# Half-height products in pairs for the down half of a perceptron, the row halves changing banks midway

## The chip, the cores and the metric

The kernel runs on one core of one Trainium2 chip, as one program. Times are microseconds of device time. The figure that counts is the median over several runs; a profile of one execution shows where the time goes.

## The reference

A token sequence of 256 with model width 1024 goes through two layers, each of a mixer (attention variants) and a perceptron, then a differential attention layer. The change lies in the perceptron, which occurs twice:

```python
def sqrelu_mlp(u, w1, w2):
    return jnp.square(jax.nn.relu(u @ w1)) @ w2
...
for layer in range(DEPTH):
    u = rms_norm(h, attn_norm[layer])
    ...
    h = h + sqrelu_mlp(rms_norm(h, mlp_norm[layer]), mlp_w1[layer], mlp_w2[layer])
```

`w1` is 1024 x 4096 and `w2` is 4096 x 1024, both float32.

## The kernel before

Precision is kept by splitting: each float32 operand becomes a high part in the format fp32r and a low part (the rest), and a product is the sum of three: high by high, high by low, low by high. TensorE does these with a stationary operand of at most 128 x 128 (LDWEIGHTS) and a moving operand of at most 512 columns (MATMUL).

All weights come as one stream of units of 128 x 1024 values. SyncE loads a unit into one of 5 slots of `raw`; ScalarE writes its high part to one of 4 slots of `wh` (`act_split`, L453), VectorE its low part to `wl` (`dve_split`, L458); TensorE uses both and counts the unit off on the semaphore `w_used`, which frees the slot.

In a perceptron (`mlp`) the 4096 hidden values are 32 blocks of 128 (`FT`). For block f, `up` (L807, L810) makes the hidden values of all 256 tokens in one PSUM bank, `ptp` or `misc` in turn, with 8 products of 512 columns and 8 of 256. ScalarE and VectorE sum, square and split them into `hh` and `hl` (128 hidden values on the partitions, 256 tokens along the free dimension). `down` then multiplies them with the block's 128 rows of `w2` and adds to the four banks `acc[2 * half + t]`: token tile t (0 or 1) by output half (512 of the 1024 columns). It is two calls of `down_part`, one for each half: for each of the two tiles three products through `mm3` (L353 high by high, L354 high by low, L355 low by high), 12 in all, each of 128 rows and 512 columns.

The order on TensorE is written out by hand: up(0), up(1), then up(f + 2), down(f) for f from 0 to 29, of which the first 10 (`TPP`) are unrolled and 20 run in a hardware loop of 2 turns (`PASSES - 1`). The last two down halves (f = 30 and 31) are issued by `down_part` directly, interleaved with what follows. `down_ready` waits for the block's weights and hidden values. In the loop a wait's value comes from a register; `at` works it out from the turn number.

Elsewhere the kernel has products that use only 64 rows of the array: the index scores (`idx_scores`, L908) and the attention scores (`ab_scores`, L944, and `pe_scores`, L424), where a head has 64 values and lies on one half of the partitions. Those have plain float32 operands; TensorE runs each as two passes with a weight load of its own.

Of the kernel before, what the change touches and what calls it, by code (L numbers as in the profile page):

```python
# [13 lines left out]
P = 128  # L14
# [45 lines left out]
SPLIT = 4  # L60
# [11 lines left out]
FT = DFF // P  # L72
# [8 lines left out]
UPS = 20  # L81
U_P = U_L + UPS - 4
UNITS = U_L + UPS * STEPS
TPP, PASSES = 10, 3
# [108 lines left out]
def at(n, i=None, per=0):  # L193

    return n if i is None else i * per + n
# [9 lines left out]
def program(nc, x, stream, consts_d, cols_d, rows_d, sel_d, out):  # L205
    with ExitStack() as ctx:  # L206
        def sb(name, shape, dt=F32):
            return ctx.enter_context(nc.sbuf_tensor(name, shape, dt))

        def sem(name):  # L210
            return ctx.enter_context(nc.semaphore(name))
# [3 lines left out]
        wh = sb("wh", [P, SPLIT, UW], F32R)  # L215
        wl = sb("wl", [P, SPLIT, UW], F32R)
# [26 lines left out]
        hh = sb("hh", [P, 2, SEQ], F32R)  # L243
        hl = sb("hl", [P, 2, SEQ], F32R)
# [13 lines left out]
        acc = [ctx.enter_context(nc.psum_tensor(f"acc{i}", [P, 512], F32)) for i in range(4)]  # L258
# [8 lines left out]
        w_hi, w_lo, w_used = sem("w_hi"), sem("w_lo"), sem("w_used")  # L267
# [8 lines left out]
        z_turned, z_act, z_dve = sem("z_turned"), sem("z_act"), sem("z_dve")  # L276
        z_cross, z_summed, sqr_done = sem("z_cross"), sem("z_summed"), sem("sqr_done")
        hid_hi, hid_lo = sem("hid_hi"), sem("hid_lo")
        act_c, dve_c, pool_c = sem("act_c"), sem("dve_c"), sem("pool_c")
        roped = sem("roped")  # L280
        a_stat, a_rstd = sem("a_stat"), sem("a_rstd")
# [69 lines left out]
        def mm3(out_, ah, al, bh, bl, start, stop_):  # L351

            nc.tensor.matmul(out_, ah, bh, start=start, stop=False, skip_group_check=True)  # L353
            nc.tensor.matmul(out_, ah, bl, start=False, stop=False, skip_group_check=True)  # L354
            return nc.tensor.matmul(out_, al, bh, start=False, stop=stop_, skip_group_check=True)  # L355
# [408 lines left out]
        def _(pe):  # L764
            mm = nc.tensor.matmul
# [24 lines left out]
            def turn_h(b, h0, cc):  # L790

                pe.wait_ge(h_done, h0 + 2 * (cc // 2) + 2)
                pe_turn_block(pe, b, h, (cc,))

            def mlp(f0, u0, b, h0, next_b, next_h0):
                def up(f, u, i=None, blocks_k=range(KD)):

                    if blocks_k[0] == 0:
                        pe.wait_ge(w_lo, at(u + 1, i, UPS))
                    if blocks_k[0] == 0 and f0 + f >= 2:  # L800
                        pe.wait_ge(z_summed, at(f0 + f - 1, i, TPP))
                    for k in blocks_k:
                        if f == 0 and k % 2 == 0:
                            pe.wait_ge(lo_out, 4 * b + k // 2 + 1)
                        ks = slice(k * P, (k + 1) * P)
                        bank = (ptp, misc)[f % 2]
                        nc.tensor.matmul(bank[:, :], wh[:, u % SPLIT, ks],  # L807
                                         xhl[:, KD + k, :, :].rearrange("p a s -> p (a s)"),
                                         start=k == 0, stop=False, skip_group_check=True)
                        last = nc.tensor.matmul(bank[:, 0:SEQ], wl[:, u % SPLIT, ks], xh[:, KD + k, :],  # L810
                                                start=False, stop=k == KD - 1, skip_group_check=True)
                    if blocks_k[-1] == KD - 1:
                        last.then_inc(w_used, 1)

                def down_part(f, u, half, tiles=range(T), opens=False):

                    ws = slice(half * 512, (half + 1) * 512)
                    for t in tiles:
                        ts = slice(t * P, (t + 1) * P)
                        last = mm3(acc[2 * half + t][:, :], hh[:, f % 2, ts], hl[:, f % 2, ts],  # L820
                                   wh[:, u % SPLIT, ws], wl[:, u % SPLIT, ws], opens, f == FT - 1)
                    return last

                def down_ready(f, u, i=None):
                    pe.wait_ge(w_lo, at(u + 1, i, UPS))
                    pe.wait_ge(hid_lo, at(f0 + f + 1, i, TPP))

                def down(f, u, i=None):

                    down_ready(f, u, i)  # L830
                    down_part(f, u, 0, opens=f == 0)
                    down_part(f, u, 1, opens=f == 0).then_inc(w_used, 1)

                up(0, u0, blocks_k=range(4))
                turn_h(b, h0, 2)
                turn_h(b, h0, 3)
                up(1, u0 + 1, blocks_k=range(4))
                for ks in (range(4, 6), range(6, KD)):
                    up(0, u0, blocks_k=ks)
                    up(1, u0 + 1, blocks_k=ks)  # L840
                for f in range(TPP):
                    up(f + 2, u0 + 2 + 2 * f)
                    down(f, u0 + 3 + 2 * f)
                with pe.Fori(0, PASSES - 1) as i:
                    for f in range(TPP, 2 * TPP):
                        up(f + 2, u0 + 2 + 2 * f, i)
                        down(f, u0 + 3 + 2 * f, i)
                u = u0 + 2 * FT - 2
                down_ready(FT - 2, u)
                down_part(FT - 2, u, 0)  # L850
                down_ready(FT - 1, u + 1)
                down_part(FT - 1, u + 1, 0).then_inc(half_summed, 1)
                down_part(FT - 2, u, 1).then_inc(w_used, 1)
                down_part(FT - 1, u + 1, 1, (0,))
                turn_h(next_b, next_h0, 0)
                down_part(FT - 1, u + 1, 1, (1,)).then_inc(w_used, 1)
                turn_h(next_b, next_h0, 1)
# [10 lines left out]
            for cc in range(4):  # L868
                pe.wait_ge(x_in[cc // 2], 32)
                for c in range(2):  # L870
                    for t in range(T):
                        f = (2 * cc + c) * P
                        last = nc.tensor.transpose(opening[cc][:, c * SEQ + t * P:c * SEQ + (t + 1) * P],
                                                   h[:, t, f:f + P], ident)
# [200 lines left out]
            for k in range(4):  # L1075
                kv, uu = divmod(k, 2)
                u = U_CMP + k
                pe.wait_ge(w_lo, u + 1)
                for j in range(8):
# [3 lines left out]
                    last = mm3(misc[0:CG * N_CMP, kv * P:(kv + 1) * P], xw_h[:, cs], xw_l[:, cs],  # L1083
                               wh[:, u % SPLIT, ws], wl[:, u % SPLIT, ws],
                               uu == 0 and j == 0, uu == 1 and j == 7)
# [1561 lines left out]
```

## Time and profile before

| | |
|---|---|
| median of 3 runs | 913.39 us (913.18 to 915.85) |
| span of the profiled execution | 912.6 us, that is 0.8 us below the median |
| TensorE busy | 892.9 us, 98% |
| VectorE, ScalarE, GpSimd busy | 650.9, 515.4, 134.8 us (71%, 56%, 15%) |
| DMA | 146.40 MB, 160 GB/s mean |
| products on TensorE | 4781, each with a weight load |

The profile gives no time of the profiled execution other than its span. Matmuls are pipelined: the time shown for one is longer than the distance from one start to the next, and it is this distance that adds up. PE is TensorE's stream of products, PEld its weight loads.

### The profile page before, as it was taken

Reading aid. Unit: us, or ns where it says so; the run is one execution under the profiler, and the core shown is the slowest. Engines: PE = TensorE matmul, PEld = TensorE weight load, DVE = VectorE, ACT = ScalarE, POOL = GpSimd, SP = SyncE. Lnnn points to the kernel's source line nnn. Section 1 sums busy time; section 2 is a strip of 40 time slices with the busy share of each in tenths; the row PEclk is TensorE's granted clock in tenths of the full one; section 3 lists DMA queues with packets and bytes.
Section 4 is the critical chain, followed back from the end, with each engine's and each line's share of the span. In section 5 each row is a group of like instructions: output and inputs, shape, how many; then the busy total and the mean of one; then the engine's idle time right before and its main releaser. Section 6 shows DMA issues by size and latency. Waiting matters only on the chain. (4 is left out here: it accounts for less than half of the span.)

```text
span 912.6 us, 14857 instructions
## 1 busy us (share of the span) xinstructions
PE 892.9 (98%) x4781; PEld 738.5 (81%) x4781; DVE 650.9 (71%) x1306; ACT 515.4 (56%) x1019; POOL 134.8 (15%) x186
## 2 busy tenths in 40 slices
PE   8999999999999999998999999999999999999998
PEld 6878788888888888787888888888887778878876
DVE  4768757666666689787576666666887878777785
ACT  6653836444444466666464444444656766666573
POOL 2310300000000010365210000000430401400401
PEclk9999999999999999999999999999999999999999
DMA  9743144655555557101446555555464345454531
GB/s 353 237 148 110 39 148 155 201 194 188 185 184 189 190 173 233 46 2 47 141 141 222 189 185 185 187 192 192 142 208 162 137 140 169 153 177 148 161 116 47
DMA packets 40953, 146.40 MB, mean 160 GB/s; under 512 B 4544, under 2 KB 5056, under 8 KB 40896
## 3 DMA queue, kind: packets, MB, share of 16 engines
q1 hardware_dynamic: 40608, 145.43, 47.3%
q8 instruction: 34, 0.56, 0.2%
q10 hardware_dynamic: 288, 0.22, 0.1%
q14 instruction: 23, 0.19, 0.1%
HBM read 144.59 MB, written 1.05 MB: 160 GB/s over the span
## 5 line engine op out<-in xcount | busy, mean ns | idle before, releaser
L458 DVE TENSOR_TENSOR wl<-raw,wh 128x1024 fp32r<-128x1024 f32 x269 | 330.8, 1234 | 138.8 <-ACT wh L453 133.2
L453 ACT ACTIVATE wh<-raw 128x1024 fp32r<-128x1024 f32 x270 | 284.5, 1056 | 150.6 <-PE acc L355 126.0
L353 PE MATMUL acc<-wh,xhl 128*128 128x512 f32 (+1 forms) x472 | 190.6, 404 | 1.0 <-DVE wl L458 0.7
L355 PE MATMUL acc<-wh,xhl 128*128 128x512 f32 (+1 forms) x472 | 184.5, 391 | 0.0
L354 PE MATMUL acc<-wl,xhl 128*128 128x512 f32 (+1 forms) x472 | 183.8, 390 | 0.0
L353 PEld LDWEIGHTS acc<-wh,xhl 128*128 128x128 f32 x472 | 88.7, 188 | 25.3 <-issue 8.0
L355 PEld LDWEIGHTS acc<-wh,xhl 128*128 128x128 f32 x472 | 88.6, 188 | 19.2
L354 PEld LDWEIGHTS acc<-wl,xhl 128*128 128x128 f32 x472 | 88.8, 188 | 16.4
L355 PE MATMUL acc<-wh,hl 128*128 128x512 f32 x256 | 101.1, 395 | 0.0
L354 PE MATMUL acc<-wl,hh 128*128 128x512 f32 x256 | 100.9, 394 | 0.0
L353 PE MATMUL acc<-wh,hh 128*128 128x512 f32 x256 | 100.9, 394 | 0.0
L807 PE MATMUL ptp<-xhl,wh 128*128 128x512 f32 x256 | 91.0, 396 | 0.7 <-DVE hr L2012 0.7
L807 PE MATMUL misc<-xhl,wh 128*128 128x512 f32 x256 | 90.7, 395 | 0.0
L810 PE MATMUL ptp<-xhl,wl 128*128 128x256 f32 x256 | 71.0, 277 | 0.0
L810 PE MATMUL misc<-xhl,wl 128*128 128x256 f32 x256 | 70.9, 277 | 0.0
L502 POOL TENSOR_SCALAR st<-st 128x2 f32<-128x2 f32 x7 | 2.7, 386 | 420.4 <-ACT o_tok L495 243.6
L807 PEld LDWEIGHTS ptp<-xhl,wh 128*128 128x128 f32 x256 | 48.0, 187 | 13.0 <-issue 1.2
L353 PEld LDWEIGHTS acc<-wh,hh 128*128 128x128 f32 x256 | 47.9, 187 | 11.8
L355 PEld LDWEIGHTS acc<-wh,hl 128*128 128x128 f32 x256 | 47.9, 187 | 11.6
L807 PEld LDWEIGHTS misc<-xhl,wh 128*128 128x128 f32 x256 | 48.0, 187 | 11.3
L354 PEld LDWEIGHTS acc<-wl,hh 128*128 128x128 f32 x256 | 47.9, 187 | 8.9
L810 PEld LDWEIGHTS ptp<-xhl,wl 128*128 128x128 f32 x256 | 48.1, 188 | 1.4
(301 smaller groups left out, 1316.1 us busy)
## 6 DMA issues: line engine op xcount, KB each, us to landing
raw<-stream SPq DMA_DIRECT2D x270, 512.0 KB, 3.3
h<-x SPq DMA_DIRECT2D x4, 256.0 KB, 4.8
out<-h SPq DMA_DIRECT2D x3, 256.0 KB, 2.1
row<-rows SPq DMA_DIRECT2D x1, 700.0 KB, 11.2
probs<-sel SPq DMA_DIRECT2D x1, 512.0 KB, 10.1
cst<-consts SPq DMA_DIRECT2D x1, 507.0 KB, 9.5
out<-h SPq DMA_DIRECT2D x2, 128.0 KB, 2.0
col<-cols ACTq DMA_DIRECT2D x1, 154.5 KB, 4.1
```

The lines of the kernel that those rows point to most:

```text
L353: nc.tensor.matmul(out_, ah, bh, start=start, stop=False, skip_group_check=True)
L354: nc.tensor.matmul(out_, ah, bl, start=False, stop=False, skip_group_check=True)
L355: return nc.tensor.matmul(out_, al, bh, start=False, stop=stop_, skip_group_check=True)
L453: nc.scalar.activation(wh[:, u % SPLIT, :], raw[:, u % RAW, :], ACT.Copy).then_inc(w_hi, 1)
L458: nc.vector.tensor_tensor(wl[:, u % SPLIT, :], raw[:, u % RAW, :], wh[:, u % SPLIT, :].bitcast(F32), ALU.subtract).then_inc(w_lo, 1)
L502: chain_link(nc.gpsimd.tensor_scalar(dst, src, 1.0 / width, EPS, ALU.mult, ALU.add))
L807: nc.tensor.matmul(bank[:, :], wh[:, u % SPLIT, ks], xhl[:, KD + k, :, :].rearrange("p a s -> p (a s)"), start=k == 0, stop=False, skip_gr ...
L810: last = nc.tensor.matmul(bank[:, 0:SEQ], wl[:, u % SPLIT, ks], xh[:, KD + k, :], start=False, stop=k == KD - 1, skip_group_check=True)
```

## The change

`down` no longer calls `down_part`. The block's 128 hidden values are cut into rows 0 to 63 and 64 to 127, and each product into two of half the height. Of a pair, one runs on the array's lower rows for one token tile, the other on the upper rows for the other tile, into different banks. For each output half that makes three pairs (one for each of the three parts). After both output halves (`swap` 0), the row halves change tiles (`swap` 1), so that every tile gets both its halves of the sum. Before a row half adds to a bank that the other wrote, a wait on the new semaphore `part_done` sees to it that those products are complete. Such waits stand at the head of each of the four groups of six products: for swap 1 on the group two before, for swap 0 on the block before (on `w_used` for its second half, and for f = 0 none). `stop` is False throughout; `start` is set on the first products into each bank.

```diff
+        part_done = sem("part_done")
...
                 def down(f, u, i=None):
 
                     down_ready(f, u, i)
-                    down_part(f, u, 0, opens=f == 0)
-                    down_part(f, u, 1, opens=f == 0).then_inc(w_used, 1)
+                    before = (f0 // FT) * 3 * (FT - 2) + 3 * f
+                    for swap in range(2):
+                        for half in range(2):
+                            if swap == 1 or (f > 0 and half == 0):
+                                pe.wait_ge(part_done, at(before + (half + 1 if swap else 0), i, 3 * TPP))
+                            elif f > 0:
+                                pe.wait_ge(w_used, at(u - 1, i, UPS))
+                            for part, (x_, w_) in enumerate(((hh, wh), (hh, wl), (hl, wh))):
+                                for r in range(2):
+                                    t = r ^ swap
+                                    rows = slice(64 * r, 64 * r + 64)
+                                    last = mm(acc[2 * half + t][:, :], x_[rows, f % 2, t * P:(t + 1) * P],
+                                              w_[rows, u % SPLIT, half * 512:(half + 1) * 512],
+                                              start=f == 0 and part == 0 and swap == 0, stop=False,
+                                              skip_group_check=True)
+                            last.then_inc(w_used if swap == 1 and half == 1 else part_done, 1)
```

## Rows read from the trace of the kernel before

**Rows 1.** The page: span, busy time by engine, and slices of the span.
```profile
span 912.6 us, 14857 instructions
...
PE 892.9 (98%) x4781; PEld 738.5 (81%) x4781; DVE 650.9 (71%) x1306; ACT 515.4 (56%) x1019; POOL 134.8 (15%) x186
...
PEclk9999999999999999999999999999999999999999
```

**Rows 2.** Groups (busy, mean ns | idle before), 145 to 328 us; TensorE's wait (us, times, longest).
```profile
L458 DVE TENSOR_TENSOR wl<-raw,wh 128x1024 fp32r<-128x1024 f32 x64 | 78.3, 1225 | 39.8 <-ACT wh L453 38.0
...
L355 PE MATMUL acc<-wh,hl 128*128 128x512 f32 x128 | 50.5, 395 | 0.0
...
L353 PE MATMUL acc<-wh,hh 128*128 128x512 f32 x128 | 50.4, 394 | 0.0
...
PE ptp L807 <- DVE hr L2012: 0.3, 1, 0.3
```

**Rows 3.** Timeline of TensorE (start, duration in us), 202.5 to 206 us: one down half.
```profile
202.94 0.28 PE L810 MATMUL misc<-xhl,wl 128*128 128x256 f32 x1
203.06 0.39 PE L353 MATMUL acc<-wh,hh 128*128 128x512 f32 x1
203.28 0.39 PE L354 MATMUL acc<-wl,hh 128*128 128x512 f32 x1
...
205.85 0.40 PE L807 MATMUL ptp<-xhl,wh 128*128 128x512 f32 x1
```

**Rows 4.** Timeline of TensorE, 48.35 to 49.5 us: into `idx_scores`.
```profile
48.38 0.39 PE L354 MATMUL acc<-wl,xhl 128*128 128x512 f32 x1
48.61 0.39 PE L355 MATMUL acc<-wh,xhl 128*128 128x512 f32 x1
48.93 0.37 PE L908 MATMUL pair<-QK 64*128 64x128 f32 x1
48.94 0.37 PE L908 MATMUL misc<-QK 64*128 64x128 f32 x1
49.14 0.27 PE L908 MATMUL pair<-QK 64*128 64x128 f32 x1
...
49.25 0.38 PE L908 MATMUL pair<-QK 64*128 64x256 f32 x1
```

**Rows 5.** Timeline of the weight loads at the same place.
```profile
48.93 0.18 PEld L908 LDWEIGHTS pair<-QK 64*128 64x128 f32 x1 [0.35 <-issue]
48.93 0.18 PEld L908 LDWEIGHTS misc<-QK 64*128 64x128 f32 x1
49.03 0.19 PEld L908 LDWEIGHTS pair<-QK 64*128 64x128 f32 x1
```

**Rows 6.** Timeline of TensorE, 87 to 89 us: into and out of `ab_scores`.
```profile
87.01 0.33 PE L939 MATMUL acc<-decay,selr 128*128 128x256 f32 x1
87.27 0.37 PE L944 MATMUL pair<-QK 64*128 64x128 f32 x1
...
87.60 0.38 PE L944 MATMUL pair<-QK 64*128 64x256 f32 x1
...
87.82 0.38 PE L944 MATMUL pair<-QK 64*128 64x256 f32 x1
...
88.13 0.50 PE L353 MATMUL acc<-wh,xhl 128*128 128x512 f32 x1
88.46 0.40 PE L354 MATMUL acc<-wl,xhl 128*128 128x512 f32 x1
```

**Rows 7.** Timeline of TensorE, 67.44 to 68.2 us: transposes, then products.
```profile
67.22 0.60 PE L417 MATMUL pair<-cst,Y 128*128 128x128 f32 x4
67.58 0.48 PE L353 MATMUL acc<-wh,xhl 128*128 128x512 f32 x1
67.89 0.40 PE L354 MATMUL acc<-wl,xhl 128*128 128x512 f32 x1
```

**Rows 8.** Timeline of ScalarE, 202.5 to 203.4 us.
```profile
203.25 0.39 ACT L1442 ACTIVATE probs<-misc 128x256 f32<-128x256 f32 x1 [1.41 <-PE misc L810]
```

## The prediction

> **What bounds the kernel now.** I read the page first. TensorE is busy 98% of the span and its granted clock is 9 tenths or more in every slice, while VectorE is at 71% and ScalarE at 56% [rows 1]. So TensorE sets the pace; what has to be asked is whether that holds in the two perceptron stages, because an average can hide a stage with another limit. The groups of one perceptron (145 to 328 us) answer it: the three products of the down half stand there with 128 instructions each and no idle time before them [rows 2]. VectorE's costliest group there, the low part of the weights, has itself waited 39.8 us, nearly all for ScalarE's high part. TensorE's own waits in that stretch add up to 0.3 us [rows 2]. Here every nanosecond added to TensorE's stream lengthens the run, and every one taken away shortens it, up to the slack of the others.
>
> The timeline then gives the price of a down half. Its 12 products start at 203.06 us and the next up half starts at 205.85 [rows 3]: 2.79 us, or 233 ns for 512 columns. A product's shown duration, 0.39 us, is its way through the array, not its rate: the next starts after 0.23. I count starts, never durations.
>
> **What changes.** In 30 of the 32 hidden blocks of each perceptron (10 written out, 2 x 10 in the loop), so 60 times in all, `down` issues 24 half-height products in place of 12 full-height ones. The last two blocks keep `down_part`. Weight loads double from 12 to 24 and four waits come in. No transfer, no ScalarE, VectorE or GpSimd instruction changes.
>
> *The streaming.* Each half-height product streams as many columns as a full one, so 24 of them take the time of 12 only if two run at once. The kernel already has such pairs: in `idx_scores` the two heads of a pair lie on the two row halves. There the products of `pair` and `misc` start 0.01 us apart, and each next one 0.11 us later for 128 columns [rows 4] and 0.22 for 256 [rows 6]; their weight loads run two at once as well [rows 5]. So concurrency is real, and two loads every 0.11 us are sustained. But those are f32 products that take a column in about 0.86 ns (0.22 us over 256), against 0.455 ns (233/512) in the down half. Two streams at the full rate never occur in this trace. From below, nothing lets a pair be done before one full-height product would be: the least that I give it is the clock, 512 columns at 2.4 GHz, 213 ns. From above, if the two streams exclude each other at that rate, a pair takes 2 x 233 = 466. I take 233, since the f32 pairs show no mutual slowing whatever, and the 20 ns above 213 then stay. The term is 12 x 233 - 12 x 233 = 0. At best 12 x 60 x 20 ns = 14.4 us are gained; by exclusion 12 x 60 x 233 ns = 168 us are lost. In other words, nothing in the streaming is saved by design: the array's area times time is the same.
>
> *The change of height.* This is what I think decides. It happens twice in each new down half. Going in: the last full-height product before `idx_scores` starts at 48.61, its forerunner at 48.38 (0.23 apart), but the first half-height pair only at 48.93, so 0.32 instead of 0.23: 0.09 us. That pair then holds its place until 49.14, 0.21 us for 128 columns, where the following 128 columns take 0.11: 0.10 us [rows 4]. The weight loads tell why: the first is at 48.93, together with its product, whereas from the second on the load stands 0.11 us ahead of its product (49.03 for 49.14) [rows 5]. Not one weight load crosses the change of height, so the array empties and the load lies bare. Going out: the last half-height products start at 87.82, a pass of 256 columns as the one from 87.60, so the next was due at 88.04; it starts at 88.13 (0.09), and lasts until 88.46, 0.33 instead of 0.23 or 0.24 (0.10) [rows 6]. Both changes together: 0.09 + 0.10 + 0.09 + 0.10 = 0.38 us, and 0.01 for the second half that starts later. Another place gives an upper value for going in: from 87.01 to 87.27 after 256 columns, the width of the up half's last product, 0.26 where the up half shows 0.12 [rows 3, 6], so 0.14 in place of 0.09; part of it is that product's own wait for weights (it lasts 0.33, not 0.28). I take 0.39 per block, with 0.44 as upper end.
>
> Is it the height, and not the number format that changes at the same places? The last f32 transposes at full height, four from 67.22 at 0.11 each, run into an fp32r product at 67.58 and a next one at 67.89 [rows 7]. The transposes need until 67.66 and the product 0.23 more: 67.89. Format costs nothing; height does. 60 x 0.39 = 23.4 us, with nothing over it, since TensorE has no idle time in which to hide it.
>
> The Trainium skill speaks both ways here. "TensorEngine Tiling (Array Packing)", section Tiling Modes, holds against the change: going from one mode to another drains TensorE. "TensorE: Matmul & The Clock Gate", section Part 1, holds for it: a weight load is drawn ahead of running products if it goes to the background buffer. By the second, the two bare loads of 0.10 would vanish, 12 us of the 23.4, and the run would take 925; [rows 5] show the first load bare, so the trace sides with the first rule and I keep the whole.
>
> *The waits.* Each group of six products (three pairs) is followed by another on different banks, and the third one waits for the first. From the last pair of a group to the weight load of the group that waits lie three pairs, 0.70 us. A 256-column product that starts at 202.94 with 0.28 us shown is read by ScalarE at 203.25 [rows 3, 8]: the shown end plus 0.03. For 512 columns that makes 0.39 + 0.03 = 0.42 us, 0.28 less than 0.70. The two waits at the head of the down half look at a whole up half or more before. What is queued behind a waiting weight load is all of TensorE's stream, but the load is not due yet when it is released. TensorE's queue can also fill fast enough: a pair's four instructions, two loads and two products, go out every 0.11 us for 128 columns [rows 4, 5], and the new pairs have 0.23. I take nothing. If the queue does not run ahead past a wait, the two waits midway cost up to 0.42 - 0.23 = 0.19 us for the product to finish and 0.10 for the bare load, 0.29 each: 60 x 2 x 0.29 = 35 us.
>
> *Who is late next.* Slots of `wh` and `wl` come free 0.39 us later per block, but TensorE needs them 0.39 later too. VectorE, which waited already [rows 2], waits longer. Nothing is given back.
>
> Sum: 23.4 us on a profiled span of 912.6, 936.0. The median of the runs lies 0.8 above the span, so 936.8; I say 937.
>
> **Rivals.**
> *The streams hinder each other.* For it: no row shows two at 0.455 ns a column. Against it: f32 pairs go undisturbed, in separate banks. Full exclusion gives 913.4 + 23.4 + 168 = 1105; half of that, 1021. Chance 0.11.
> The Trainium skill, "TensorE: Matmul & The Clock Gate", section Part 3, gives 3.07x for four row tiles at 512 columns. An estimate from that page alone, a pair at 4/3.07 of 233 ns, would be 303 ns and 987 us in all; no row here shows it.
>
> *The waits bite.* Place: swap 1, both halves. Price up to 35 us, so 972; a third of it gives 949. It decides if a product's completion reaches the queue later than 0.70 us after its start. Chance 0.12.
>
> *The pair runs at the clock.* If the 20 ns over 213 come with the height, 14.4 us return: 922. For it: f32 pairs at 256 columns take 0.22, close to the clock. Against it: fp32r's excess is proportional to the columns, 0.12 for 256 in the up half. Chance 0.11.
>
> *No cost of the change, the other side.* Place: the first weight load of each down half and of the up half behind it, which would be drawn under the running products. Price: 23.4 us less, so 913.4, no change; with pairs at the clock 899. It decides below (2.7/60 =) 0.045 us per block. Against it: each change of height in [rows 4, 6] is paid for, while loads at one height are drawn ahead. Chance 0.06, split between no change (0.03) and faster (0.03).
>
> **How the numbers follow.** My forecast has 0.58, and the remaining 0.02 go to something unseen and slower. Being faster with the height's cost in place would need pairs below 233 - (23.4 + 2.7)/0.72 = 197 ns, under the 213 of the clock, so faster needs the last rival. A measurement of this kernel can tell about 0.3%, 2.7 us. Faster 0.03, same 0.03, slower 0.94. The range: low 922 for the pair at the clock; high 960, which takes in 0.44 per block (940) and most of the waits' cases. It leaves out the streams that hinder each other, the worst waits and the other side, some 0.2.
>
> **What would show it.** Right: a block's down half takes 3.18 us from its first product to the up half's first, not 2.79; inside it pairs 0.01 us apart, at 0.23 us; a gap of 0.09 and a first pair of 0.33 at its head, and a first up product of 0.33 behind it; TensorE's weight loads with idle time put down to "issue" there. Wrong: pairs at 0.21 or over 0.30; a stretched pair at the middle of the down half (the waits); a first weight load that starts ahead of its product. Most of all I would be wrong if two full-rate streams do not fit side by side.

## The result, and the profile after

The changed kernel takes 939.42 us (median of 4 runs, 939.18 to 939.62), beside 913.51 us for the kernel before in the same comparison. The ratio is 1.0276, with a 95% interval of 1.0259 to 1.0293. It is slower by 25.9 us. I had said 937, slower by 23.6.

The page after, answering to [rows 1]: TensorE is as full as before, at 9 tenths of its clock or more in every slice as before. The other engines have the instructions they had; VectorE and ScalarE are busy for the same time (GpSimd 136.1 us against 134.8).

```profile
span 937.4 us, 16421 instructions
...
PE 917.7 (98%) x5501; PEld 733.7 (78%) x5501; DVE 650.9 (69%) x1306; ACT 515.4 (55%) x1019; POOL 136.1 (15%) x186
...
PEclk9999999999999999999999999999999999999999
```

There are 720 products more (60 x 12) and 720 weight loads more, and the busy time shown for the loads fell from 738.5 to 733.7 us. So a count of instructions would have misled here: the two loads of a pair overlap, and the time that they share is counted once.

TensorE's timeline over one block, in time where [rows 3] are (start, shown duration in us; x2 folds two products into a row, here the two of a pair):

```profile
206.25 0.40 PE L808 MATMUL misc<-xhl,wh 128*128 128x512 f32 x1
206.49 0.28 PE L811 MATMUL misc<-xhl,wl 128*128 128x256 f32 x1
206.70 0.50 PE L843 MATMUL acc<-wh,hh 64*128 64x512 f32 x2
207.04 0.39 PE L843 MATMUL acc<-wl,hh 64*128 64x512 f32 x2
207.26 0.40 PE L843 MATMUL acc<-wh,hl 64*128 64x512 f32 x2
207.50 0.39 PE L843 MATMUL acc<-wh,hh 64*128 64x512 f32 x2
...
209.37 0.40 PE L843 MATMUL acc<-wh,hl 64*128 64x512 f32 x2
209.69 0.50 PE L808 MATMUL ptp<-xhl,wh 128*128 128x512 f32 x1
210.03 0.28 PE L811 MATMUL ptp<-xhl,wl 128*128 128x256 f32 x1
...
212.50 0.28 PE L811 MATMUL ptp<-xhl,wl 128*128 128x256 f32 x1
212.72 0.50 PE L843 MATMUL acc<-wh,hh 64*128 64x512 f32 x2
```

Read the starts. From 206.49 to the first pair it is 0.21 us, where the same step before is 0.12. The first pair holds its place for 0.34. From 207.04 to 209.37 there are ten steps of 0.233, the old pace. The duration shown for two products folded together, 0.39 or 0.40, is that of one alone, so the two of a pair start within about 0.01 us of each other. From the last pair to the up half it is 0.32, and the up half's first product holds for 0.34. The 0.50 shown for the two products behind a change, against 0.39 or 0.40, is the same delay seen from inside.

The weight loads at the head of the down half, answering to [rows 5]:

```profile
206.25 0.19 PEld L811 LDWEIGHTS misc<-xhl,wl 128*128 128x128 f32 x1
206.69 0.18 PEld L843 LDWEIGHTS acc<-wh,hh 64*128 64x128 f32 x2 [0.26 <-issue]
206.80 0.19 PEld L843 LDWEIGHTS acc<-wl,hh 64*128 64x128 f32 x2
207.04 0.19 PEld L843 LDWEIGHTS acc<-wh,hl 64*128 64x128 f32 x2
```

The load for the product of 206.49 is there at 206.25, one product ahead. The load for the first pair comes at 206.69, together with it. The next one is ahead again. Nobody is named as releaser of the 0.26 us before it: "issue" means that no other engine was waited for.

TensorE's loads over most of the first perceptron (145 to 330 us), in the view of the waits (us in total, times, longest):

```profile
PEld acc L843 <- issue: 7.8, 30, 0.3
PEld ptp L808 <- issue: 4.3, 11, 0.6
PEld misc L808 <- issue: 4.1, 11, 0.4
PEld ptp L808 <- DVE wl L459: 1.5, 4, 0.4
PEld misc L808 <- DVE wl L459: 1.5, 4, 0.4
```

The 30 idle stretches ahead of L843 are the 30 changes into the half height. The four rows below are the changes out of it (29 of them, and one stretch of 0.6 us before the first; the last change out lies just past 330 us). Two of them name VectorE for 4 changes each. The idle time is 0.37 us at every one of the 29, while VectorE's split had ended anything from 0.22 to 0.78 us before the load, so VectorE is not what was waited for.

### The profile page after: what moved, and what is told of

Same layout as the page of the kernel before. It is cut to its first block and busy times, and to the rows that moved or that the text cites. A ratio compares the mean times of both kernels' runs of the same rounds, so it can differ in the third digit from the quotient of the medians.

```text
span 937.4 us, 16421 instructions
## 1 busy us (share of the span) xinstructions
PE 917.7 (98%) x5501; PEld 733.7 (78%) x5501; DVE 650.9 (69%) x1306; ACT 515.4 (55%) x1019; POOL 136.1 (15%) x186
## 5 line engine op out<-in xcount | busy, mean ns | idle before, releaser
L843 PE MATMUL acc<-wh,hh 64*128 64x512 f32 x480 | 101.1, 418 | 0.0
L808 PE MATMUL ptp<-xhl,wh 128*128 128x512 f32 x256 | 95.2, 411 | 0.7 <-DVE hr L2027 0.6
L808 PE MATMUL misc<-xhl,wh 128*128 128x512 f32 x256 | 95.3, 411 | 0.0
L843 PE MATMUL acc<-wh,hl 64*128 64x512 f32 x480 | 95.1, 392 | 0.0
L843 PE MATMUL acc<-wl,hh 64*128 64x512 f32 x480 | 94.7, 391 | 0.0
L843 PEld LDWEIGHTS acc<-wh,hh 64*128 64x128 f32 x480 | 45.0, 184 | 23.4 <-issue 15.2
L843 PEld LDWEIGHTS acc<-wh,hl 64*128 64x128 f32 x480 | 45.0, 184 | 10.9
L843 PEld LDWEIGHTS acc<-wl,hh 64*128 64x128 f32 x480 | 45.0, 184 | 8.3
L1437 ACT ACTIVATE probs<-probs,nb 128x128 f32<-128x128 f32 (+1 forms) x96 | 42.3, 444 | 11.5 <-DVE nb L1965 11.5
```

The source lines that it names most:

```text
L808: nc.tensor.matmul(bank[:, :], wh[:, u % SPLIT, ks], xhl[:, KD + k, :, :].rearrange("p a s -> p (a s)"), start=k == 0, stop=False, skip_gr ...
L843: last = mm(acc[2 * half + t][:, :], x_[rows, f % 2, t * P:(t + 1) * P], w_[rows, u % SPLIT, half * 512:(half + 1) * 512], start=f == 0 an ...
L1437: last = s_.activation(pb[:, c0:c0 + n], pb[:, c0:c0 + n], ACT.Exp, scale=-1.0, bias=nbs[:, a, t:t + 1], accum_out=sus[:, a, t:t + 1])
```

## The experiments

Seven kernels ran. The figures of the changed kernel stand beside them: 939.42 us, ratio 1.0276. Each ratio is against the kernel before as it ran beside that experiment, 912.94 to 914.25 us, so differences between medians of two experiments are good to about 1 us.

**No change of height inside the loop.** The up half in pairs too.

```diff
                         bank = (ptp, misc)[f % 2]
+                        if f >= 2:
+                            for x_, n in ((wh, 2 * SEQ), (wl, SEQ)):
+                                for r in range(2):
+                                    rows = slice(64 * r, 64 * r + 64)
+                                    to = (bank, pair[f % 2])[r]
+                                    last = mm(to[:, 0:n], x_[rows, u % SPLIT, ks],
+                                              xhl[rows, KD + k, 0:n // SEQ, :].rearrange("p a s -> p (a s)"),
+                                              start=k == 0 and n > SEQ, stop=k == KD - 1 and n == SEQ,
+                                              skip_group_check=True)
+                            continue
```

> The down half stays as changed, and the up half of blocks 2 to 31 is cut into half-height pairs as well, the upper rows' products going to a bank of their own (pair), which nobody adds: the upper rows' half of the up sum is left out of the result. The array's height then changes only at the ends of the two perceptrons, not twice per block. If the change of height is what costs (0.39 us a block), 60 blocks give it back: 914 to 918 us, and no block shows a gap or a stretched first pair. If half-height pairs, doubled weight loads or the four waits cost something of themselves, the time stays at 939 us or rises, since there are more pairs than before and the same waits.

Measured: 915.13 us (913.42 to 921.51), ratio 1.0017 (0.9999 to 1.0036), no measurable difference from the kernel before. The down half of this kernel is the changed kernel's, with its 24 half-height products, its 24 loads and its four waits. Its timeline across the head of the down half:

```profile
203.28 0.39 PE L813 MATMUL pair<-xhl,wh 64*128 64x512 f32 x1
203.43 0.28 PE L813 MATMUL misc<-xhl,wl 64*128 64x256 f32 x1
203.51 0.28 PE L813 MATMUL pair<-xhl,wl 64*128 64x256 f32 x1
203.55 0.46 PE L853 MATMUL acc<-wh,hh 64*128 64x512 f32 x2
203.78 0.47 PE L853 MATMUL acc<-wl,hh 64*128 64x512 f32 x2
...
206.12 0.47 PE L853 MATMUL acc<-wh,hl 64*128 64x512 f32 x2
206.35 0.39 PE L813 MATMUL ptp<-xhl,wh 64*128 64x512 f32 x1
```

From 203.43 to 203.55 it is 0.12, from 203.55 to 203.78 0.23, and the whole down half takes 2.80 us (203.55 to 206.35), the 2.79 of [rows 3]. The gap and the stretched first pair are gone with the change of height. One thing about the pairs differs: their two products start 0.08 us apart, as the half-height products of the up half before them do (203.43 and 203.51), which is why 0.46 or 0.47 is shown for two. The pace is 0.233 all the same. This is the run that carries the explanation.

**Four changes of height per block instead of two.** Output half 0 at full height between the two swaps of output half 1.

```diff
+                    half = 1
+                    for swap in range(2):
+                        if swap == 1:
+                            down_part(f, u, 0, opens=f == 0)
+                            pe.wait_ge(part_done, at(before + 1, i, TPP))
+                        elif f > 0:
+                            pe.wait_ge(w_used, at(u - 1, i, UPS))
...
+                        last.then_inc(w_used if swap == 1 else part_done, 1)
```

> Only output half 1 is in half-height pairs; output half 0 stays at full height and stands between the two swaps, so a block changes height four times instead of twice, with half of the half-height products (12 of 24) and two waits fewer. If each change of height costs about 0.2 us: two more per block, 60 x 0.39 = 23 us more than the changed kernel, 963 us (960 to 967). If the cost goes with the number of half-height products, weight loads or waits, it is halved: 926 us.

Measured: 962.37 us, ratio 1.0524 (1.0507 to 1.0542): 22.95 us above the changed kernel, 0.38 us per block for two changes more. Half the half-height products and twice the changes give nearly twice the loss (5.2% against 2.8%), so the loss goes with the changes. The inner ones in its timeline:

```profile
204.57 0.40 PE L844 MATMUL acc<-wh,hl 64*128 64x512 f32 x2
204.90 0.50 PE L354 MATMUL acc<-wh,hh 128*128 128x512 f32 x1
205.25 0.39 PE L355 MATMUL acc<-wl,hh 128*128 128x512 f32 x1
...
206.17 0.40 PE L356 MATMUL acc<-wh,hl 128*128 128x512 f32 x1
206.50 0.49 PE L844 MATMUL acc<-wh,hh 64*128 64x512 f32 x2
206.83 0.40 PE L844 MATMUL acc<-wl,hh 64*128 64x512 f32 x2
```

Out: 0.33 and 0.35 where 0.23 is due; in: 0.33 and 0.33. The format is the same on both sides (fp32r), which [rows 4] and [rows 6] could not offer.

**No crossing, no waits.**

```diff
-                            if swap == 1 or (f > 0 and half == 0):
-                                pe.wait_ge(part_done, at(before + (half + 1 if swap else 0), i, 3 * TPP))
-                            elif f > 0:
-                                pe.wait_ge(w_used, at(u - 1, i, UPS))
...
-                                    t = r ^ swap
+                                    t = r
...
-                            last.then_inc(w_used if swap == 1 and half == 1 else part_done, 1)
+                    last.then_inc(w_used, 1)
```

> As changed, but the row halves keep their tiles in the second round, so no bank is ever written from both and the semaphore part_done and all four waits of a block are gone (half of each product's sum is left out and the other half counted twice). If the waits are hidden, as I forecast: 939 us, within 1.5. If they cost something: up to 35 us less, down to 905; a few us if the register arithmetic behind them is what slows the up half by the 0.05 us per block that I see in the profile and did not forecast.

Measured: 939.40 us, ratio 1.0272 (1.0255 to 1.0289). The four waits and the register arithmetic behind them cost nothing that can be measured, and they do not explain the slower up half either: in this kernel's trace it takes the same 3.02 us from its first product to the next down half.

**The swap directly behind its own group.**

```diff
-                    for swap in range(2):
-                        for half in range(2):
+                    for half in range(2):
+                        for swap in range(2):
+                            if swap == 1:
+                                pe.wait_ge(part_done, at(before + 2 * half + 1, i, 3 * TPP))
+                            elif f > 0 and half == 0:
+                                pe.wait_ge(part_done, at(before - 1, i, 3 * TPP))
...
```

> As changed, but the swap follows its own output half at once: half 0 swap 0, half 0 swap 1, half 1 swap 0, half 1 swap 1. The wait at each swap now looks at the group directly before it instead of the one before that. By my figures for a wait that is not hidden (0.42 us to completion less 0.23 of streaming, and 0.10 for the bare weight load, 0.29 each, 120 times) it is 35 us slower than the changed kernel: 974 us (962 if the weight load is not bare). If such a wait costs nothing at any distance: 939 us.

Measured: 977.86 us, ratio 1.0699 (1.068 to 1.0718), 38.4 us above the changed kernel, 0.32 per wait. Around the first of the two waits:

```profile
213.25 0.40 PE L845 MATMUL acc<-wl,hh 64*128 64x512 f32 x2
213.49 0.39 PE L845 MATMUL acc<-wh,hl 64*128 64x512 f32 x2
213.94 0.50 PE L845 MATMUL acc<-wh,hh 64*128 64x512 f32 x2
214.28 0.39 PE L845 MATMUL acc<-wl,hh 64*128 64x512 f32 x2
```

From 213.49 to 213.94 it is 0.45 where 0.23 is due (I had 0.42), then 0.34 for the bare load. So a wait on TensorE's own product costs 0.32 us if nothing stands between, and three pairs between, as in the changed kernel, hide it (in its trace the first pair behind such a wait starts at 208.20, the pair before it at 207.97, 0.23 as everywhere). Fewer than three were not tried.

**Only the lower rows' 12 products.**

```diff
+                    rows = slice(0, 64)
+                    for half in range(2):
+                        for t in range(T):
+                            for part, (x_, w_) in enumerate(((hh, wh), (hh, wl), (hl, wh))):
+                                last = mm(acc[2 * half + t][:, :], x_[rows, f % 2, t * P:(t + 1) * P],
...
```

> The down half of blocks 0 to 29 issues only its 12 products of rows 0 to 63 and leaves the upper rows' 12 products out; no waits between them. If the two row halves really run side by side at the full rate, leaving one out gains nothing, and the two changes of height are still paid: 938 us (936 to 940), slower than the kernel before with half of its arithmetic in these blocks. If the two streams cost each other something, this is faster than the changed kernel by it.

Measured: 940.69 us (939.17 to 946.4), ratio 1.0293 (1.0276 to 1.031). The median lies 0.7 us above my range of 936 to 940; the two executions at a mean clock of 1.00 took 939.17 and 939.50, the one of 946.4 had 0.991. The interval overlaps the changed kernel's (1.0259 to 1.0293). With half of the down half's arithmetic left out of 60 blocks, the kernel is still as slow as the changed one. So the upper rows' products are free beside the lower ones, and the loss comes neither from two streams side by side nor from the number of loads.

**All 24 on the lower rows.**

```diff
+                    rows = slice(0, 64)
+                    for again in range(2):
+                        for half in range(2):
+                            for part, (x_, w_) in enumerate(((hh, wh), (hh, wl), (hl, wh))):
+                                for t in range(T):
...
```

> The down half of blocks 0 to 29 issues 24 half-height products, all on rows 0 to 63 (each of the 12 twice; the upper rows are left out), with no waits between them. If concurrency on two row halves is what keeps the changed kernel's down half at 12 x 0.233 us, this one takes 24 x 0.233: 60 x 2.8 = 168 us more, 1107 us. If the array would take two products side by side on the same rows, or the number of products is not what counts: 939 us.

Measured: 1107.86 us, ratio 1.2132 (1.2112 to 1.2152), 168.4 us above the changed kernel. Two products on the same rows in the timeline:

```profile
206.59 0.62 PE L837 MATMUL acc<-wh,hl 64*128 64x512 f32 x2
207.06 0.62 PE L837 MATMUL acc<-wh,hh 64*128 64x512 f32 x2
207.53 0.62 PE L837 MATMUL acc<-wl,hh 64*128 64x512 f32 x2
```

A step of 0.47 for two, and a shown duration of 0.62 for the two together, against 0.23 and 0.39 or 0.40 for a pair on two row halves in the changed kernel: the fold of x2 in the timeline says nothing on its own about running at once, its duration and step do.

**The pairs issued apart.** Three products of the lower rows, then three of the upper, in each group.

```diff
-                            for part, (x_, w_) in enumerate(((hh, wh), (hh, wl), (hl, wh))):
-                                for r in range(2):
+                            for r in range(2):
+                                for part, (x_, w_) in enumerate(((hh, wh), (hh, wl), (hl, wh))):
```

> As changed, but inside each group of six the three products of the lower rows are issued first and then the three of the upper rows, instead of alternately. If TensorE only overlaps neighbours in its stream, each group runs five products long instead of three: 60 x 4 x 2 x 0.233 = 112 us more, 1051 us. If each row half takes its own products from what has been issued (the eight passes of two attention heads in the kernel before, issued one head after the other, last 0.93 us together, which is the time of one head's 0.11 + 0.11 + 0.22 + 0.22 with its bare start), the three products and loads that lie between do not matter: 939 us. Group to group I do not know how far the queue reaches; a partial overlap would lie between.

Measured: 939.93 us, ratio 1.0293 (1.0276 to 1.031). The issue order inside a group makes no measurable difference. The trace of it has the lower and the upper rows' product of the same part side by side:

```profile
207.38 0.39 PE L843 MATMUL acc<-wl,hh 64*128 64x512 f32 x2
207.61 0.39 PE L843 MATMUL acc<-wh,hl 64*128 64x512 f32 x2
207.84 0.40 PE L843 MATMUL acc<-wh,hh 64*128 64x512 f32 x2
```

## Why the prediction was right, point by point

*TensorE sets the pace in the perceptrons, and nothing gives time back.* Right. VectorE's and ScalarE's busy times are unchanged, and the loss in TensorE's timeline is the loss of the run.

*Two full-rate streams fit side by side.* This was the step without a row, and the one I would have been most wrong about. Right: ten steps of 0.233 us after, and the two kernels on the lower rows bracket it (leaving the upper rows out gains nothing, putting them on the lower rows costs 168.4 us where I had 168). The rival that the streams hinder each other falls. So does the pair at the clock: its pace is that of a full-height product, 0.233, neither 0.21 nor the 0.30 of the prediction's estimate.

*The change of height, 0.39 us per block.* Right in mechanism, in place and in each of the four pieces, which the timeline after gives as 0.09 + 0.11 + 0.09 + 0.11 = 0.40. Shown by taking it away (915.13 us) and by doubling it (962.37 us). The format cannot be the cause, since it is fp32r on both sides of every one of these changes. The rival without this cost falls with the loads of L843, none of which is ahead of its first pair. The rule of the Trainium skill that this rival goes with, that a weight load is drawn ahead if it goes to the background buffer, stands in "TensorE: Matmul & The Clock Gate" under Part 2, not Part 1. Inside one height this trace agrees (load at 206.25 for the product at 206.49); across the change no load was drawn ahead (206.69 for 206.70).

*The waits, nothing.* Right, by the kernel without them (939.40 us). The rival's price was nearly right as well, 38.4 us against 35, but for an order of groups that this change does not have.

*The sum.* Low by 2.4 us in the median: 937 against 939.42, or 23.4 us of loss against 25.9. A block took 5.57 us before (203.06 to the next block's 208.63) and takes 6.02 after (206.70 to 212.72): 0.45, not 0.39. The part beyond the four pieces lies in the up half. From its second product to its end, the gap of the next change taken off, it is 212.72 - 210.03 - 0.09 = 2.60 us after, and 208.63 - 205.85 - 0.23 = 2.55 before. I took the streaming of everything but the changes as it was; this 0.05 us per block, 3 us in all, is the term that I left out. The waits do not cause it. In the traces of all six experiments that keep the change of height the up half is as long as in the changed kernel, 3.02 us from its first product to the next down half, whatever stands in the down half; where the up half is in half-height pairs too, it is 2.78, as before the change. So the 0.05 comes with the change of height, and the cost of the two changes was mis-sized by it. It is not simply paid by every full-height product behind a change: in the kernel with four changes the four steps from 205.25 to 206.17 are at 0.23. Its cause stays open.

Sixty blocks at 0.45 would be 27 us, but the two profiles differ by 24.8. From the last down product of the first perceptron to the first up product of the second it was 138.15 us before (323.12 to 461.27), and it is 136.59 after (336.00 to 472.59). The profile of before had a stretch at half clock there, 1.2 instead of 2.4 GHz (us; busy us and instructions of PE, PEld, DVE, ACT, POOL; clock, DMA):

```profile
422.00:423.00 1.00, 1.00 (x8) 0.70 (x6) 1.00 (x4) 0.37 (x1) 0.92 (x3) 0.50 0.00 0
423.00:424.00 1.00, 1.00 (x6) 0.48 (x3) 1.00 (x2) 0.00 (x0) 1.00 (x1) 0.50 0.00 0
```

Just before, from 419 to 420 us, TensorE had been busy for 0.18 of the microsecond. The changed kernel's profile had no such stretch in the whole of this part:

```profile
336.00:472.59 136.59, 129.24 (x861) 110.08 (x859) 105.24 (x283) 86.25 (x216) 43.28 (x76) 1.00 0.34 108
```

The 1.56 us between the two are of the size that a stretch at half clock from 422 to 425 us costs, and 24.8 + 1.56 = 26.4 is close to the 27. It lies outside the change. It also bent a term of the forecast: I took the median as 0.8 us above the span of the profile, but that span held this stretch; after the change, without one, the median is 2.0 above it (939.42 and 937.4). Two single executions should not be compared to the microsecond without looking at the clock.

*One sign was wrongly set.* I wrote that a down half would take 3.18 us from its first product to the up half's first. It takes 2.99 (206.70 to 209.69), because only two of the four pieces lie between those starts: 2.79 + 0.10 + 0.09 = 2.98. The gap going in comes before, the up half's bare load after. The sum of the prediction does not use the 3.18.

## What to carry to other kernels

Cutting full-height products into half-height pairs buys nothing where the full height was already in use, since a pair takes as long as the one product it replaces. What it costs is the change of height: 0.2 us each time, in a gap of 0.09 and a bare weight load (one that is not drawn ahead) of 0.10, which could be read beforehand from the places where the kernel does it already. If half-height products are needed for their own sake, put them next to each other, or keep all of a loop at one height, and let a wait on TensorE's own product have three products of 512 columns between, as here; less was not tried.

## What the runs showed of the hardware that was not expected

The row halves take their products from what has been issued ahead, not only from neighbours in the stream: three lower and then three upper products with their loads ran as pairs (939.93 us; 1051 would have been program order).

Behind a change of height the up half keeps a slightly slower pace from its second product to its end, 2.60 us against 2.55. The kernel with only the lower rows' 12 products, which has no waits between them, shows the same 2.60: its up half goes from the second product at 210.22 to the next down half at 212.91, less the gap of 0.09.

```profile
210.22 0.28 PE L811 MATMUL ptp<-xhl,wl 128*128 128x256 f32 x1
...
212.91 0.50 PE L836 MATMUL acc<-wh,hh 64*128 64x512 f32 x1
```
